# State tables doubled by ScalarE products and weight splits moved ahead of side work, in a two-block sequence model on one core

## The reference, cut to what matters

```python
proj = rmsnorm(x, norm_pre) @ w_in              # 512 x 2048 @ 2048 x 5120
u_s, g_s, q_d, k_d, v_d, g_d, q_x, g_x = split(proj)
# state space part: 64 groups of 64 complex states
dt = exp(log_dt);  abar = exp((a_re + 1j * a_im) * dt)
x_t = abar * x_{t-1} + (z * B) u_t;   y_t = Re(C x_t) + D u_t
# ... differential attention, memory attention, then w_out
# then a second model of two layers whose shift, scale and gate come from silu(c) @ ada_w
```

## Time and profile before

| | |
|---|---|
| median of 3 runs | 3290.7 us (3290.01 to 3291.89) |
| the profiled execution | 3289.22 us |
| its span, first to last instruction | 3287.4 us |
| mean granted TensorE clock | 0.937 |
| busy: PE / DVE / ACT / POOL | 89% / 53% / 24% / 16% |
| opening (to about 145 us) and state space stage (about 145 to 680 us) | the two stages that the change touches |

### The profile page before, as it was taken

How to read it: one execution, slowest core, us unless ns; L and a number is a source line. 1 busy time by engine, 2 the same in 40 slices (tenths; PEclk the granted TensorE clock), 3 DMA queues, 4 the chain that set the end, 5 groups by cost and what they waited for, 6 DMA issues and landing times. The chain is left out here.

```text
span 3287.4 us, 35120 instructions
## 1 busy us (share of the span) xinstructions
PE 2939.9 (89%) x13768; PEld 2205.4 (67%) x13768; DVE 1758.0 (53%) x2107; ACT 786.9 (24%) x1019; POOL 531.4 (16%) x411
## 2 busy tenths in 40 slices
PE   6999999987559958999999988899949999989897
PEld 4756666675228837888888765588828877765585
DVE  6799999965653365112553237522272157337433
ACT  4311111133432222111222213311122122213221
POOL 3365565515010041000000001000030000001000
PEclk8999999998679977999999999999959999999998
DMA  4667877761023141222433332222113254341321
GB/s 161 216 264 297 317 285 295 294 247 56 26 103 118 51 179 41 85 80 103 163 117 119 115 124 75 108 76 88 62 58 106 95 193 157 136 158 60 144 90 63
DMA packets 112852, 454.03 MB, mean 138 GB/s; under 512 B 11472, under 2 KB 20816, under 8 KB 76752
## 3 DMA queue, kind: packets, MB, share of 16 engines
q1 hardware_dynamic: 112720, 452.24, 37.5%
HBM read 380.36 MB, written 71.83 MB: 138 GB/s over the span
## 5 line engine op out<-in xcount | busy, mean ns | idle before, releaser
L2302 PE MATMUL ps<-h_hi,w_hi 128*128 128x512 f32 (+1 forms) x1792 | 661.6, 369 | 78.8 <-POOL h_lo L490 72.8
L2303 PE MATMUL ps<-h_lo,w_hi 128*128 128x512 f32 (+1 forms) x1792 | 645.0, 360 | 0.0
L2304 PE MATMUL ps<-h_hi,w_lo 128*128 128x512 f32 (+1 forms) x1792 | 640.8, 358 | 0.0
L2302 PEld LDWEIGHTS ps<-h_hi,w_hi 128*128 128x128 f32 x1792 | 344.9, 192 | 151.9 <-POOL h_lo L490 51.7
L384 PE MATMUL ps<-h_hi,w_hi 128*128 128x512 f32 (+1 forms) x1152 | 413.0, 358 | 37.7 <-DVE w_lo L337 37.7
L385 PE MATMUL ps<-h_lo,w_hi 128*128 128x512 f32 (+1 forms) x1152 | 412.2, 358 | 0.0
L2186 DVE TENSOR_TENSOR w_lo<-raw,w_hi 128x2048 fp32r<-128x2048 f32 x72 | 164.8, 2289 | 460.6 <-ACT w_hi L2137 460.6
L386 PE MATMUL ps<-h_hi,w_lo 128*128 128x512 f32 (+1 forms) x1152 | 410.0, 356 | 0.0
L2303 PEld LDWEIGHTS ps<-h_lo,w_hi 128*128 128x128 f32 x1792 | 346.1, 193 | 51.9 <-issue 6.0
L2304 PEld LDWEIGHTS ps<-h_hi,w_lo 128*128 128x128 f32 x1792 | 344.9, 192 | 51.3
L1475 POOL TENSOR_TENSOR wide<-ident_sb,stat 128x128 f32<-128x128 f32 x96 | 38.5, 401 | 1454.2 <-DVE stat L1535 1454.2
(11 more groups left out here) (305 smaller groups left out, 4333.7 us busy)
## 6 DMA issues: line engine op xcount, KB each, us to landing
raw<-w_in SPq DMA_DIRECT2D x112, 1024.0 KB, 5.1
raw<-ada_w SPq DMA_DIRECT2D x96, 1024.0 KB, 9.1
raw<-w_out SPq DMA_DIRECT2D x48, 1024.0 KB, 5.0
proj<-xw SPq DMA_DIRECT2D x60, 384.0 KB, 2.5
xw<-proj SPq DMA_DIRECT2D x70, 256.0 KB, 3.2
xw<-proj SPq DMA_DIRECT2D x46, 384.0 KB, 3.2
xw<-resid SPq DMA_DIRECT2D x8, 1536.0 KB, 12.2
proj<-wide SPq DMA_DIRECT2D x32, 256.0 KB, 11.2
```

The source lines that it names most:

```text
L2302: pe.matmul(a_[q], wh, h_hi[:, k, a:b], start=k == 0, stop=False)
L2303: pe.matmul(a_[q], wh, h_lo[:, k, a:b], start=False, stop=False)
L2304: ins = pe.matmul(a_[q], wl, h_hi[:, k, a:b], start=False, stop=k == KC - 1)
```

## The change

It has four parts. (1) In the opening, x comes in two queues: groups 0 and 2 from SP's, 1 and 3 from ACT's; ACT runs a `Sqrt` on one column ahead of the squares, which puts the load of that function table there. (2) DVE's splits stand one piece of side work earlier; the split of tile 2 and its wait on PE go in two halves; ACT's squares of the memory come in turn 7 in place of turn 6. (3) The state tables: POOL copies the 32 fine powers and then doubles the table four times (32 to 64, ..., 256 to 512 columns). For each doubling ACT makes the four products with a column of `e_sb` as its scale into `gt`, and POOL the difference and the sum. ACT does this for slot n+1 between `w_hi(n)` and `out_(n-1)`. (4) SP waits for the opening's stores at the start of the next block.

```diff
@@ opening
+                    act.wait_ge(m2.h, m2.at(1))
+                    act.activation(stat[:, 20:21], lam[:, 7:8], ACT.Sqrt)
                     for k in range(KC):
@@ ACT and DVE, tile 2 (ACT's part; DVE and PE wait on half_hi, half_lo in the same way)
+                        if n == 2:
+                            act.wait_ge(half_used.h, half_used.at(1))
+                            act.activation(w_hi[:, 0, 0:D // 2], raw[:, 0, 0:D // 2], ACT.Copy).then_inc(half_hi.h, 1)
+                            act.wait_ge(w_used.h, w_used.at(1))
+                            act.activation(w_hi[:, 0, D // 2:D], raw[:, 0, D // 2:D], ACT.Copy).then_inc(hi_done.h, 1)
+                            return
...
-                        if n == 6:
+                        if n == 7:
                             for k in range(KC):
@@ DVE
+                    low(2)
                     for n in range(2, tiles):
-                        low(n)
+
+                        if n + 1 < tiles:
+                            low(n + 1)
@@ ssm_and_conditions, POOL
+                        er, ei = ee[n % 2]
+
+                        pool.wait_ge(x_ready.h, x_ready.at(n - 1))
+                        pool.tensor_copy(er[:, 0:S_FINE], e_sb[:, j, 0, 0:S_FINE]).then_inc(st.step(), 1)
+                        pool.tensor_copy(ei[:, 0:S_FINE], e_sb[:, j, 1, 0:S_FINE]).then_inc(st.step(), 1)
                         pool.wait_ge(st.sem, st.now)
...
+                        for s in range(4):
+                            m = S_FINE << s
+                            pool.wait_ge(turn_in.h, turn_in.at(4 * n + s + 1))
+                            pool.tensor_tensor(er[:, m:2 * m], gt[0][:, 0:m], gt[1][:, 0:m], ALU.subtract).then_inc(st.step(), 1)
+                            pool.wait_ge(st.sem, st.now)
+                            pool.tensor_tensor(ei[:, m:2 * m], gt[2][:, 0:m], gt[3][:, 0:m], ALU.add).then_inc(
+                                st.tell(e_ready, n + 1) if s == 3 else st.tell(turn_out, 3 * n + s + 1), 1)
+                            pool.wait_ge(st.sem, st.now)
@@ ssm_and_conditions, ACT
+                    def table(n):
+
+                        i, j = divmod(n, 4)
+                        if j == 0:
+                            act.wait_ge(loaded[1].h, loaded[1].at(16 * (i + 1)))
+                        for s in range(4):
+                            m = S_FINE << s
+                            a = S_FINE + (1 << s)
+                            w_re, w_im = e_sb[:, j, 0, a:a + 1], e_sb[:, j, 1, a:a + 1]
+                            er, ei = (e_sb[:, j, c, 0:S_FINE] if s == 0 else ee[n % 2][c][:, 0:m] for c in range(2))
+                            if s:
+                                act.wait_ge(turn_out.h, turn_out.at(3 * n + s))
+                            else:
+                                act.wait_ge(e_ready.h, e_ready.at(n))
+                            act.activation(gt[0][:, 0:m], er, ACT.Copy, scale=w_re)
+                            act.activation(gt[1][:, 0:m], ei, ACT.Copy, scale=w_im)
+                            act.activation(gt[2][:, 0:m], er, ACT.Copy, scale=w_im)
+                            act.activation(gt[3][:, 0:m], ei, ACT.Copy, scale=w_re).then_inc(turn_in.h, 1)
+                    table(0)
                     for n in range(slots):
...
                         act.activation(w_hi[:, n % 2, :], raw[:, 0, :], ACT.Copy).then_inc(hi_done.h, 1)
+                        if n + 1 < slots:
+                            table(n + 1)
```

More of the change, by code:

```diff
@@ L532, in _ @@
                     sp.dma_start(cv[:], cp).then_inc(m1.h, 16)
-                    for g in range(4):
-                        sp.dma_start(xw[:, 4 * g * T:4 * (g + 1) * T], x_in[:, 4 * g:4 * g + 4, :].rearrange("p k n -> p (k n)")
-                                     ).then_inc(loaded[g].h, 16)
+                    for g in (0, 2):
+                        load_x(sp, g)
                     for n in range(2):
@@ L573, in _ @@
                         sp.dma_start(proj[n], stg[n % 2]).then_inc(stored[n % 2].h, 16)
-                    for q in range(2):
-                        sp.wait_ge(stored[q].h, stored[q].at(16 * tiles // 2))
                     sp.wait_ge(mix_in.h, mix_in.at(32))
@@ L579, in _ @@
                 def _(act):
+                    for g in (1, 3):
+                        load_x(act, g)
                     credit(act, 0)
@@ L737, in low @@
                     def low(n):
+                        if n == 2:
+                            dve.wait_ge(half_hi.h, half_hi.at(1))
+                            dve.tensor_tensor(w_lo[:, 0, 0:D // 2], raw[:, 0, 0:D // 2], w_hi[:, 0, 0:D // 2].bitcast(F32),
+                                              ALU.subtract).then_inc(half_lo.h, 1)
+                            dve.wait_ge(hi_done.h, hi_done.at(3))
+                            dve.tensor_tensor(w_lo[:, 0, D // 2:D], raw[:, 0, D // 2:D], w_hi[:, 0, D // 2:D].bitcast(F32),
+                                              ALU.subtract).then_inc(lo_done.h, 1)
+                            return
                         dve.wait_ge(hi_done.h, hi_done.at(n + 1))
@@ L842, in step @@
                     def step(n, k):
+                        if n == 2 and k == 0:
+                            pe.wait_ge(half_lo.h, half_lo.at(1))
+                        elif k == 0 or (n == 2 and k == KC // 2):
+                            pe.wait_ge(lo_done.h, lo_done.at(n + 1))
                         if k == 0:
-                            pe.wait_ge(lo_done.h, lo_done.at(n + 1))
                             pe.wait_ge(staged.h, staged.at(n - 3))
@@ L859, in step @@
                             ins.then_inc(w_used.h, 1)
+                        elif n == 0 and k == KC // 2 - 1:
+                            ins.then_inc(half_used.h, 1)
                     lead = 5
@@ L899, in ssm_and_conditions @@
             ee = [[take(T) for _ in range(2)] for _ in range(2)]
-            gt = [take(T) for _ in range(3)]
+            gt = [take(T // 2) for _ in range(4)]
             t = [take(T) for _ in range(4)]
@@ L917, in _ @@
                         i, j = divmod(n, 4)
+                        if n == 0:
+                            for q in range(2):
+                                sp.wait_ge(stored[q].h, stored[q].at(0))
                         if j == 0 and i:
@@ L965, in _ @@
                             pool.wait_ge(loaded[1].h, loaded[1].at(16 * (i + 1)))
[L966 to L970, removed]
@@ L979, in _ @@
-                        pool.wait_ge(st.sem, st.now)
-                        pool.tensor_tensor(g_[1], f_im, c_re, ALU.mult).then_inc(st.step(), 1)
-                        pool.wait_ge(st.sem, st.now)
-                        pool.tensor_tensor(ee[n % 2][1], gt[2], gt[1], ALU.add).then_inc(st.tell(e_ready, n + 1), 1)
+                        er, ei = ee[n % 2]
+                        pool.wait_ge(x_ready.h, x_ready.at(n - 1))
+                        pool.tensor_copy(er[:, 0:S_FINE], e_sb[:, j, 0, 0:S_FINE]).then_inc(st.step(), 1)
@@ L1140, in ssm_and_conditions @@
             for s, v in ((loaded[0], 32 * chunks), (loaded[1], 16 * chunks), (loaded[2], 16 * chunks), (b_ready, slots // 2),
-                         (b_read, slots), (e_ready, slots), (x_ready, slots), (y_out, chunks), (pair_used, slots // 2), (ada_used, per * slots), (ada_copied, 3 * LAYERS),
+                         (b_read, slots), (e_ready, slots), (turn_in, 4 * slots), (turn_out, 3 * slots), (x_ready, slots), (y_out, chunks), (pair_used, slots // 2), (ada_used, per * slots), (ada_copied, 3 * LAYERS),
                          (ada_turned, 3 * LAYERS), (mods_done, 3 * LAYERS), (hi_done, slots), (lo_done, slots),
```

14 lines of the change are left out of this document (7 added, 7 removed).

## The result

The changed kernel takes 3395.71 us in the median of four runs (3390.17 to 3398.49), beside 3290.36 for the kernel before (3284.63 to 3291.89): a ratio of 1.032, with an interval of 1.030 to 1.034. It is slower by 105 us. The forecast was slower by 45, with a range up to 3370; rival (4), 3370 to 3400, had 0.08.

A forecast was written before the change was run, and what follows sets the result against it. PE was taken to bound the state space stage: floor 459.6 + stalls 35 + clock 10.5 + 4.2 = 509.3 against 468.0, +41.3. With the start +4 and the opening +0.8 that made +46, 3335 us, range 3300 to 3370.

The forecast's parts named there:

- rival (4): State tables: POOL's small operations and the handovers cost twice the price, every odd slot waits, 3370 to 3400; chance 0.08.
- floor, slot 2 to 31: State space stage, slot 2 to 31: PE's own work with five transpositions takes 459.6 us.
- stalls ahead of slots 3, 7, ..., 27: Each chunk's last slot: PE waits 5.0 us for `out_` behind the table that needs `ssm_e`, 7 x 5.0 = 35 us.
- stalls ahead of slots 5, 9, ..., 29: Other odd slots: `out_` waits for a table gated by `x_ready`, 0.6 in each of seven slots, 4 us.
- half clock behind the waits: Chunks' last slots: after the 5 us wait the clock falls, costing 7 x 1.5 = 10.5 us (0 to 19).
- opening: Before the state space stage: the changed head costs 0.8 us (-1.5 to +2.5), the reordered splits 0.
- A0: Table chain: ACT's first group of four products, 32 columns each, takes 1.06 us.
- half speed: Upper bound for chunks' last slots: POOL at half speed beside DVE and a later landing, 8.3 us a chunk.
- the landing: Chunk's last slot: the load of `ssm_e` lands 16.7 us after ACT starts `out_` of slot 4i-3.
- the gain is given back at the sum: 0: Opening: time saved before tiles 2 and 3 is lost again as PE waits for `add_mem` before its memory sum.
- x in two queues has the same bytes behind it: Head of the opening: splitting x over two queues adds no load time; the head costs +0.8 us in all.
- (1): State space stage: `ssm_e` and the table come in time for `out_`, PE at its floor, 3282 to 3286; chance 0.12.

The follow-up runs named there:

- experiment 1: The changed kernel with `out_(n-1)` ahead of the table of slot n+1 on ACT: 3280.57 us, ratio 0.9977.
- experiment 6: The changed kernel, but in odd slots DVE waits for the next slot's table before its split: 3428.68 us, one run.
- Experiment 3: The changed kernel with two buffers for the table factors, so that `ssm_e` is loaded earlier: 3380.49 us, ratio 1.0278.
- experiment 9: The kernel before with the changed opening, but all of x from SP's queue and no early `Sqrt`: 3290.32 us, ratio 1.0003.
- experiment 10: The kernel before with one edit, groups 1 and 3 of x issued from ACT's queue: 3295.08 us, ratio 1.0021.
- 7: The opening of the changed kernel with the state space stage of before: 3290.93 us, ratio 1.0009.
- experiment 8: The changed kernel's opening with the stage of before, but all of x from SP's queue: 3290.00 us, ratio 1.0002.
- experiment 5: The changed kernel with `out_(n-1)` ahead of the table's last four products, behind the first twelve: 3327.52 us, ratio 1.0122.

## Why the prediction was wrong

The sign, the place and the mechanism were right: PE bounds the stage, `out_` behind the table stalls it, released by `out_`, and the clock falls behind the wait. The size was less than half. Measured against the sum's terms:

| term | forecast | measured |
|---|---|---|
| floor, slot 2 to 31 | 459.6 | 459.3 (experiment 1) |
| stalls ahead of slots 3, 7, ..., 27 | 35 | 46 |
| stalls ahead of slots 5, 9, ..., 29 | 4.2 | 34 |
| half clock behind the waits | 10.5 | 26 |
| start, to slot 2 | 4 | 7.2 |
| opening | 0.8 | 3.5 |

**The step that failed** is "0.6 in each of seven slots, 4 us (0 to 15)", the stalls ahead of slots 5, 9, ..., 29: measured 4.8 in each, 34 us. It was the difference of two sums of about 21 us, 21.0 against 20.5, and the first of them was 25.2 (395.26 to 420.49). It had two terms wrong.

The first is `x_ready`. It came 13.3 us behind W (395.26 to 408.58) and not 12.0. I took DVE's 10.0 us from slot 31, an odd one. In an even slot DVE's turn back waits for `state_out`, which stands behind a quarter of PE's tile. Slot 12, from DVE's timeline:

```profile
404.75 0.69 DVE L1121 TENSOR_TENSOR xw<-xw 128x512 f32<-128x512 f32 x1 [1.39 <-PE ps L1147]
```

PE's stalls don't make this wait: experiment 1, where PE has none, has it as well (220 to 640 us):

```profile
DVE xw L1121 <- PE ps L1147: 14.5, 13, 1.4
```

The second is the chain from `x_ready` to PE's start, 11.9 and not 9.0. DVE beside POOL makes it 3.5 longer (experiment 6). In these slots, the second of a chunk, the copy of the state outputs (L1027) also stands between the table and `out_`, 0.5 us that I had not counted. And ACT's first four products, A0, are not in it. They don't wait for `x_ready` and are through ten microseconds before it; I had them in the chain with 1.06:

```profile
397.55 0.31 ACT L1047 ACTIVATE xw<-xw 128x32 f32<-128x32 f32 x1
...
419.29 0.57 ACT L1027 ACTIVATE wide<-ps 128x512 f32<-128x512 f32 x1
```

3.5 + 0.5 - 1.1 is the 2.9 between 11.9 and 9.0. Each of these slots then has the clock's loss too, which was counted for seven slots only: 14 x 1.85 = 26 in place of 7 x 1.5.

**The reason under most of it** was the price of POOL. I had seen that POOL is slower beside DVE and set POOL's small operations at their undisturbed price for the likely case, with half speed as the upper bound. Experiment 6 shows that the undisturbed price was right, and that it doesn't hold here: in the 11.2 us of the chain of slot 13 DVE works for 11.0 (over the stage it is 65%, and 97% before). The bound "half speed" was of the wrong form: an operation that ends with DVE's instruction doesn't scale with POOL's columns.

**The block at the chunk's end** was mis-sized by 11 us: the landing was right (16.6 for 16.7 in the mean), the chain behind it 10.5 for 8.7, with POOL's operations of 32 to 128 columns again beside DVE. Experiment 3 shows that the landing was only the last of two gates 2 us apart.

**The start:** table 0 ahead of the first `w_hi` (PE's first matmul 7.4 later, 3.5 of them the opening's), and then what I had not counted: slot 0 at half clock for its first part (12.79 us for 11.20), and slot 1 waiting for `out_(0)` behind table 2 (a gap of 9.94 for 9.01).

**The opening:** "the gain is given back at the sum: 0" held (experiment 9). "x in two queues has the same bytes behind it" was wrong: the last bytes do come as before, but the first group that ACT needs comes 4.8 us later, behind group 1. It costs 5 us; the early `Sqrt` gives 1.5 of them back (rms at 27.40 in experiment 10, 25.86 in 7; POOL's end at 150.42 and 148.96), since ACT waits for x anyway, and nothing once x is early (22.75 in experiment 8, 22.59 in 9).

**The rivals.** (4) named what happened, POOL's small operations well above their price and a wait in every odd slot, and its time. Its other half, the handovers, is small: in experiment 6 they take 0.04 us from POOL to ACT and 0.14 from ACT to POOL, priced 0.06. A chance of 0.08 was too little for a case whose main condition, POOL slower beside DVE, the rows of before showed (1.81 against 1.29). (1) did not come true in this kernel, but its floor can be had with all these tables once `out_` stands ahead of them (experiment 1).

## What to carry to other kernels

An instruction for which the bounding engine waits belongs ahead of any chain that goes back and forth between two other engines; moved by a few lines, the same work made this stage 96 us longer or 9 shorter. Where a forecast hangs on the difference of two large sums, price both kinds of outcome, with everything that follows from the worse one (here the clock), and take each term from a slot of the same kind (an even slot of DVE has a wait that an odd one has not). Price a small POOL operation by the DVE instruction that it may start in, not by its columns alone. And when a stream of loads is split over two queues, read in which order the pieces land: here the piece that was needed first came second.

## What was not expected of the hardware

- A POOL copy of 32 columns takes 0.21 us alone and 2.32 beside a DVE subtraction of 2.29 us: it ends with DVE's instruction. A sum of 128 columns took 1.25 in a scan of DVE and 0.46 beside an idle DVE. Beside DVE's products with one input from PSUM the copy takes 0.21 all the same.
- Whether the clock falls isn't told by the length of the gap alone. In experiment 5 gaps of 3.2 to 3.6 us left the 48 matmuls at 11.1 us each time; gaps of 4.93 and 6.22 left them at 11.2, while one of 5.10 made them 12.7.
- With the four groups of x split over two queues, group 1 landed at 6.3 us and group 0 at 10.7, where all four from one queue land in order from 5.9 on.
